# Two products of 256 columns become one of 512 in the cross attentions' key and query projections

## What is computed

```python
def memory_cross_attention(xn, mem, mem_gain, wq, wkv, wo):
    mn = rms_norm(mem, mem_gain)
    q = jnp.einsum('bsd,de->bse', xn, wq)            # 1024 -> 512, 4 heads of 128
    k, v = jnp.split(jnp.einsum('bmd,de->bme', mn, wkv), 2, axis=-1)
    s = jnp.einsum('bqhd,bkhd->bhqk', q, k) * (XA_HEAD_DIM ** -0.5)
    p = jax.nn.softmax(s, axis=-1)
    o = jnp.einsum('bhqk,bkhd->bqhd', p, v)
    return jnp.einsum('bse,ed->bsd', o, wo)

# reference(): for each of the 2 layers, behind the even or the odd mixer
x = x + memory_cross_attention(rms_norm(x, xa_norm[layer]), mem, xa_mem_norm[layer],
                               xa_wq[layer], xa_wkv[layer], xa_wo[layer])
```

## Time and profile before

| | us |
|---|---|
| median of 3 runs | 592.36 (592.31 to 592.51) |
| the profiled execution | 592.32 |
| its span in the trace | 590.5 |
| outside the span | 1.8 |
| PE busy | 578.7 (98%) |
| PE weight loads busy | 533.7 (90%) |
| DVE busy | 415.5 (70%) |
| ACT busy | 390.6 (66%) |

### The profile page before, as it was taken

The page is one execution under the profiler, slowest core; times in us unless marked ns, Lnnn a source line. Parts: engine busy times, 40 slices in busy tenths (PEclk is TensorE's granted clock), DMA queues, the critical chain, the costliest instruction groups (busy, mean ns, idle before and its releaser), DMA issues.

```text
span 590.5 us, 9701 instructions
## 1 busy us (share of the span) xinstructions
PE 578.7 (98%) x3879; PEld 533.7 (90%) x3879; DVE 415.5 (70%) x639; ACT 390.6 (66%) x587; POOL 62.2 (11%) x55
## 2 busy tenths in 40 slices
PE   7999999999999999999999999999999999999995
PEld 6999989999999898889988999999899998788984
DVE  6779589447855784567557874788998973776664
ACT  7763685278367875657666847769849828566754
POOL 7230005001001000100000001104120200100002
PEclk9999999999999999999999999999999999999999
DMA  9756354445715563464335555236544563256201
GB/s 286 251 182 224 102 184 143 143 143 214 229 58 172 165 235 142 159 231 181 143 144 170 186 172 187 85 137 224 189 150 144 181 239 132 93 213 231 89 1 71
DMA packets 51980, 97.83 MB, mean 166 GB/s; under 512 B 1372, under 2 KB 7776, under 8 KB 51936
## 3 DMA queue, kind: packets, MB, share of 16 engines
q1 hardware_dynamic: 51392, 96.87, 48.2%
q10 hardware_dynamic: 160, 0.27, 0.1%
q0 software_dynamic: 384, 0.08, 0.1%
HBM read 96.16 MB, written 1.05 MB: 165 GB/s over the span
## 4 chain that ended last, share of the span: by engine, by line
PE 80%; ACT 7%; DVE 6%; DVEq 2%; ACTq 2%; issue 1%; DMA 1%
PE proj L1705 13%; PE proj L1707 13%; PE proj L1706 13%; PE proj L1724 9%; PE proj L1726 9%; PE proj L1725 9%; PE head L1874 3%; DVE w_lo L1040 3%; ACT w_hi L476 2%; PE head L1952 1%; PE head L1762 1%; DVEq L1552 1%; ACT z_silu L514 1%; ACTq L516 1%; DVE v_rows L1501 1%
## 5 line engine op out<-in xcount | busy, mean ns | idle before, releaser
L1040 DVE TENSOR_TENSOR w_lo<-raw_weights,w_hi 128x1024 fp32r<-128x1024 f32 x174 | 227.5, 1321 | 108.1 <-ACT w_hi L476 105.7
L476 ACT ACTIVATE w_hi<-raw_weights 128x1024 fp32r<-128x1024 f32 x176 | 184.5, 1057 | 113.5 <-PE proj L1707 59.9
L1705 PE MATMUL proj<-xT_hi,w_hi 128*128 128x256 f32 x760 | 218.2, 287 | 0.2 <-DVE w_lo L1111 0.2
L1707 PE MATMUL proj<-xT_hi,w_lo 128*128 128x256 f32 x760 | 215.0, 283 | 0.0
L1706 PE MATMUL proj<-xT_lo,w_hi 128*128 128x256 f32 x760 | 215.0, 283 | 0.0
L1705 PEld LDWEIGHTS proj<-xT_hi,w_hi 128*128 128x128 f32 x760 | 145.7, 192 | 1.0 <-issue 0.3
L1706 PEld LDWEIGHTS proj<-xT_lo,w_hi 128*128 128x128 f32 x760 | 145.8, 192 | 0.6
L1707 PEld LDWEIGHTS proj<-xT_hi,w_lo 128*128 128x128 f32 x760 | 145.7, 192 | 0.0
L1724 PE MATMUL proj<-w_hi,y_hi 128*128 128x512 f32 x176 | 69.6, 396 | 0.5 <-DVE w_lo L1040 0.5
L1726 PE MATMUL proj<-w_lo,y_hi 128*128 128x512 f32 x176 | 68.6, 390 | 0.0
L1725 PE MATMUL proj<-w_hi,y_lo 128*128 128x512 f32 x176 | 68.5, 389 | 0.0
(11 more groups left out here) (277 smaller groups left out, 750.7 us busy)
## 6 DMA issues: line engine op xcount, KB each, us to landing
raw_weights<-in_ev_w_in_dram SPq DMA_DIRECT2D x15, 2048.0 KB, 8.8
raw_weights<-in_od_w_in_dram SPq DMA_DIRECT2D x12, 2048.0 KB, 8.0
raw_weights<-in_ev_w_out_dram SPq DMA_DIRECT2D x4, 2048.0 KB, 7.7
raw_weights<-in_xa_wkv_dram SPq DMA_DIRECT2D x4, 2048.0 KB, 7.8
raw_weights<-in_od_w_out_dram SPq DMA_DIRECT2D x4, 2048.0 KB, 7.7
raw_weights<-in_xa_wq_dram SPq DMA_DIRECT2D x2, 2048.0 KB, 9.0
raw_weights<-in_xa_wo_dram SPq DMA_DIRECT2D x2, 2048.0 KB, 7.8
raw_weights<-in_ev_w_in_dram SPq DMA_DIRECT2D x4, 512.0 KB, 7.9
```

The costliest lines, as they stand in the source:

```text
L476: act.activation(ring_quarter(w_hi, n, q), raw_quarter(n, q), ACT.Copy).then_inc(hi_ready, 1)
L1040: dve.tensor_tensor(ring_quarter(w_lo, n, q), raw_quarter(n, q), ring_quarter(w_hi, n, q).bitcast(F32), ALU.subtract).then_inc(lo_ready, 1)
L1705: pe.matmul(dst, wh[:, k, :], x_hi[:, k, :], start=(k == 0), stop=False)
L1707: last = pe.matmul(dst, wl[:, k, :], x_hi[:, k, :], start=False, stop=(k == KC - 1))
```

## The change

The key and query slabs of both cross attentions (four slabs) become "paired". The two parts of x lie side by side in one tensor, and for each block PE does one product of 512 columns, w_hi with x_hi and x_lo, into the two halves of a bank, and one of 256 columns, w_lo with x_hi, into the first half. So a quarter fills a whole bank, and a key slab takes four banks instead of two. The sum of the two halves is made by DVE (`tensor_reduce` over an innermost axis of 2) when the bank is read; ACT's copies of keys and queries are gone. The sums stand in DVE's order behind the `ahead` step of the same place.

```diff
+PAIRED = {("XA0", "k"), ("XA0", "q"), ("XA1", "k"), ("XA1", "q")}
...
-        _t += 2 if _kind == "W" or (_stage[:2] == "XA" and _part == "q") else 1
+        _t += 2 if _kind == "W" or is_paired(_n) else 1
...
+        xT = sb("xT", [P, 2, KC, S], F32R)
+        xT_hi, xT_lo = xT[:, 0], xT[:, 1]
...
-                copy_bank(nk, 0, kx[:, 0:2, :].rearrange("p h t -> p (h t)"), k_rows)
...
-                copy_bank(nk, 1, kx[:, 2:4, :].rearrange("p h t -> p (h t)"), k_rows)
...
-                    query(nq, h)
...
+            def pair_sum(n, half, dst, s):
+
+                filled(dve, n, 0, half)
+                dve.tensor_reduce(dst, two_banks(n, half).rearrange("p u (l t) -> p u t l", l=2), AX_X, ALU.add
+                                  ).then_inc(s, 1)
+                dve.drain().then_inc(free_of(n, 0, half), 1)
+                dve.nop().then_inc(free_of(n, 1, half), 1)
+
+            def keys_sum(n, half):
+                pair_sum(n, half, kx[:, 2 * half:2 * half + 2, :], k_rows)
+
+            def query_sum(n, h):
+
+                dve.wait_ge(quarter_used, 4 * n + h + 1)
+                dve.tensor_reduce(blocks(0)[:, h, :], bank(n, h % 2, h // 2).rearrange("p (l t) -> p t l", l=2), AX_X,
+                                  ALU.add).then_inc(q_rows, 1)
+                dve.drain().then_inc(free_of(n, h % 2, h // 2), 1)
...
-                for q in range(1, 4):
-                    ahead(nk, q)
+                ahead(nk, 1)
+                ahead(nk, 2)
+                keys_sum(nk, 0)
+                ahead(nk, 3)
                 xT_low(1, "xa_norm", 0)
                 ahead(nq, 0)
+                keys_sum(nk, 1)
                 ahead(nq, 1)
+                query_sum(nq, 0)
                 ahead(nq, 2)
+                query_sum(nq, 1)
                 softmax_max(8 + 1, 0, False)
                 ahead(nq, 3)
+                query_sum(nq, 2)
                 softmax_max(8 + 2, 1, False)
                 softmax_norm(16 + 2, 0, False)
                 ahead(nv, 0)
+                query_sum(nq, 3)
                 softmax_max(8 + 3, 2, False)
...
                 ahead(nq, 0)
+                query_sum(nq, 0)
+                ahead(nq, 1)
+                query_sum(nq, 1)
                 softmax_max(12 + 1, 0, False)
-                ahead(nq, 1)
                 softmax_norm(24 + 2, 0, False)
                 softmax_max(12 + 2, 1, False)
                 ahead(nq, 2)
+                query_sum(nq, 2)
                 softmax_max(12 + 3, 2, False)
                 softmax_norm(24 + 4, 1, False)
                 softmax_norm(24 + 6, 2, False)
+                query_sum(nq, 3)
                 cross_low(11, 0)
...
+                    if paired and k < KC - 1:
+                        pe.matmul(both, wh[:, k, :], x_pair[:, :, k, :], start=(k == 0), stop=False)
+                        pe.matmul(dst, wl[:, k, :], x_hi[:, k, :], start=False, stop=False)
```

More of the change, by code:

```diff
@@ L66, in slab, with is_paired @@
     return [n for n, s in enumerate(SLABS) if s[0] == stage and s[1] == part and s[3] == g][0]
+PAIRED = {("XA0", "k"), ("XA0", "q"), ("XA1", "k"), ("XA1", "q")}
+def is_paired(n):
+    return SLABS[n][:2] in PAIRED
 TURN = {}
@@ L96, in hybrid_trunk @@
         w_lo = sb("w_lo", [P, 4, 1024], F32R)
[L97 to L100, removed]
+        xT = sb("xT", [P, 2, KC, S], F32R)
+        xT_hi, xT_lo = xT[:, 0], xT[:, 1]
+        y = sb("y", [P, 2, 2 * KC, S], F32R)
+        y_hi, y_lo = y[:, 0], y[:, 1]
         x_sb = sb("x_residual", [P, T, D])
@@ L141, in hybrid_trunk @@
         kx = scan_mask[:, :].rearrange("p (h t) -> p h t", h=4)
-        proj = [ctx.enter_context(nc.psum_tensor(f"proj{i}", [P, 512], F32)) for i in range(4)]
+        proj_banks = ctx.enter_context(nc.psum_tensor("proj", [P, 4, 512], F32))
+        proj = [proj_banks[:, i, :] for i in range(4)]
         head = [ctx.enter_context(nc.psum_tensor(f"head{i}", [P, 512], F32)) for i in range(4)]
@@ L300, in filled, with two_banks @@
                 return
-            eng.wait_ge(quarter_used, 4 * n + (2 * u + 2 if kind == "F" else 2 * half + 2 if kind == "W" else 4))
+            eng.wait_ge(quarter_used, 4 * n + (2 * half + 2 if kind == "W" or is_paired(n) else
+                                               2 * u + 2 if kind == "F" else 4))
+        def two_banks(n, half):
+            b = 2 * ((TURN[n] + half) % 2)
+            return proj_banks[:, b:b + 2, :]
         def y_src(i):
@@ L708, in cross_high @@
                                ACT.Copy).then_inc(y_hi_ready, 1)
[L710 to L713, removed]
             def first_cross():
@@ L769, in last_cross @@
                 cross_high(1, 0)
-                query(nq, 3)
                 turned_probs(12 + 3, 2, 512)
@@ L840, in _ @@
             ahead(n, 2)
-            copy_bank(n, 0, kx[:, 0:2, :].rearrange("p h t -> p (h t)"), k_rows)
             ahead(n, 3)
@@ L894, in stage_c @@
                     silu_of_c(0)
-                else:
-                    n = slab("XA1", "k")
-                    copy_bank(n, 1, kx[:, 2:4, :].rearrange("p h t -> p (h t)"), k_rows)
                 ahead(cx, 1)
@@ L1484, in _ @@
             norm_rows(3, x_sb, W[:, 0:2, :])
-            for q in range(1, 4):
-                ahead(n, q)
+            ahead(n, 1)
+            ahead(n, 2)
+            keys_sum(n, 0)
+            ahead(n, 3)
             xT_low(2, "od_norm", 0)
@@ L1529, in stage_c @@
                 ahead(cx, 0)
+                if g == 0:
+                    keys_sum(slab("XA1", "k"), 1)
                 ahead(cx, 1)
@@ L1687, in take_bank, with quarter_f @@
                     pe.wait_ge(free_of(n, u, half), before)
-            def quarter_f(n, q, x_hi=xT_hi, x_lo=xT_lo, norm=None, four_banks=False, ks=range(KC)):
-                if four_banks:
+            def quarter_f(n, q, x_pair=xT, norm=None, ks=range(KC)):
+                x_hi, x_lo = x_pair[:, 0], x_pair[:, 1]
+                paired = is_paired(n)
+                if paired:
                     u, half, col = q % 2, q // 2, 0
@@ L1700, in quarter_f @@
                 dst = bank(n, u, half)[:, col:col + S]
+                both = bank(n, u, half).rearrange("p (a t) -> p a t", a=2)
                 wh, wl = ring_quarter(w_hi, n, q), ring_quarter(w_lo, n, q)
@@ L1704, in quarter_f @@
                         pe.wait_ge(xT_lo_ready, KC * norm + k + 1)
-                    pe.matmul(dst, wh[:, k, :], x_hi[:, k, :], start=(k == 0), stop=False)
-                    pe.matmul(dst, wh[:, k, :], x_lo[:, k, :], start=False, stop=False)
-                    last = pe.matmul(dst, wl[:, k, :], x_hi[:, k, :], start=False, stop=(k == KC - 1))
+                    if paired and k < KC - 1:
+                        pe.matmul(both, wh[:, k, :], x_pair[:, :, k, :], start=(k == 0), stop=False)
+                        pe.matmul(dst, wl[:, k, :], x_hi[:, k, :], start=False, stop=False)
+                    elif paired:
+                        pe.matmul(dst, wl[:, k, :], x_hi[:, k, :], start=False, stop=False)
+                        last = pe.matmul(both, wh[:, k, :], x_pair[:, :, k, :], start=False, stop=True)
+                    else:
+                        pe.matmul(dst, wh[:, k, :], x_hi[:, k, :], start=(k == 0), stop=False)
+                        pe.matmul(dst, wh[:, k, :], x_lo[:, k, :], start=False, stop=False)
+                        last = pe.matmul(dst, wl[:, k, :], x_hi[:, k, :], start=False, stop=(k == KC - 1))
                 if ks[-1] == KC - 1:
@@ L1746, in last_products, with slab_f @@
                     last.then_inc(last_filled, 1)
-            def slab_f(n, qs=range(4), x=(xT_hi, xT_lo), norm=None):
+            def slab_f(n, qs=range(4), x_pair=xT, norm=None):
                 for q in qs:
-                    quarter_f(n, q, x[0], x[1], norm=norm if q == 0 else None)
+                    quarter_f(n, q, x_pair, norm=norm if q == 0 else None)
             def slab_t(n, qs=range(4), x=(xT_hi, xT_lo), k0=0, start=True, stop=True):
@@ L1975, in first_cross @@
                 pe.wait_ge(mn_lo_ready, KC)
-                slab_f(nk, [0, 1, 2], x=(y_hi, y_lo))
+                slab_f(nk, [0, 1, 2], y)
                 turn_rows(W[:, 0:2, :], 2)
-                slab_f(nk, [3], x=(y_hi, y_lo))
+                slab_f(nk, [3], y)
                 for q in range(4):
-                    quarter_f(nq, q, norm=1 if q == 0 else None, four_banks=True)
+                    quarter_f(nq, q, norm=1 if q == 0 else None)
                     if q >= 1:
@@ L2006, in query @@
                 def query(q, ks=range(KC)):
-                    quarter_f(nq, q, norm=3 if q == 0 else None, four_banks=True, ks=ks)
+                    quarter_f(nq, q, norm=3 if q == 0 else None, ks=ks)
                 query(0)
@@ L2047, in _ @@
             pe.wait_ge(mn_lo_ready, 2 * KC)
-            slab_f(slab("XA1", "k"), [0, 1, 2], x=(y_hi, y_lo))
+            slab_f(slab("XA1", "k"), [0, 1, 2], y)
             turn_rows(W[:, 0:2, :], 3)
```

(2 more changed lines are left out.)

3 lines of the change are left out of this document (removed).

## The result

The changed kernel takes 594.96 us (median of 6 runs, 594.77 to 595.22), the kernel before 592.39 us beside it (592.31 to 592.71). The ratio is 1.0041 with a 95% interval of 1.0031 to 1.0052: slower by 2.6 us. The forecast was 594.8 us.

A forecast was written before the change was run, and what follows sets the result against it. PE, busy for 98% of the span, was taken to bound the kernel. First cross attention +1.0, second layer's keys +0.25 and last cross attention +1.15 gave +2.4 us on 592.32: 594.7, forecast 594.8, range 592.4 to 598.0.

The forecast's parts named there:

- a query sum, a key sum: DVE's new reductions: 0.68 us per query quarter, 1.22 us per pair of key banks, taken from the lower bound.
- score 0, first layer: First cross attention: the query sum queues behind DVE work, so PE stalls 0.8 us and starts this score at 287.11.
- score 3, first layer: First cross attention's second stall: sum queued behind softmax and `w_lo`; start 298.93 instead of 298.02, PE at +1.0 us with restart.
- PE at score 2, last layer: Last cross attention: query sum behind a `w_lo` ends at 563.64; score starts 0.84 us later, +0.94 with restart.
- and at score 3: Last cross attention: DVE's sum takes 0.68 us instead of ACT's 0.38, 0.2 us later; +1.15 us for this layer.
- The slow reduction: Rival: one more cycle per output, sums of 0.95 and 1.75 us; some +3.2 us more, 598 us; 17%.
- The restart: At scores that waited, restarting costs PE another 0.1 us: 1.13 us against 1.03.
- PE's gain: Key and query slabs: one 512-column product replaces two of 256, saving 13.3 ns per block, 1.7 us in all.
- Second layer's keys: First key sum delays `xT_low`, so PE waits at C x: the slab's 0.43 us gain lost and 0.25 more.
- PE's waits would name `xT_low` here: Sign: PE's waits name `xT_low` before C x in the second layer; the prediction is wrong if missing.
- Stages C and D: Their chain through ACT and DVE, some 50 us, starts from PE's end of C z and only moves along.

The follow-up runs named there:

- the kernel that sums nothing: Changed kernel with all four slabs paired, but DVE sums nothing and ACT copies only the first half of each bank: 591.47 us, ratio 0.9987.
- the quarters sorted by width: Reordered kernel with the last query quarter as before the change, plus whole quarters' products ordered by width instead of alternating: 591.74 us.
- XA1 k: Only the second layer's key slab is paired, the other three slabs as in the kernel before: ratio 1.0026 against that kernel.
- The reordered kernel: Changed kernel with DVE's query sums moved ahead of `w_lo` steps of the same place, and second-layer `xT_low` ahead of the third `w_lo`: 591.75 us, ratio 0.9987.
- another kernel with the same beginning: Changed kernel with each of the eight query sums done twice, one behind the other: 601.01 us.
- three kernels: Kernel before with one slab paired: first layer's keys, first layer's queries, or second layer's keys; ratios 1.0014, 1.0064 and 1.0026.
- a fourth: Kernel before with only the second layer's query slab paired: ratio 1.0026.

## Why the prediction was right

The chain of the argument held, from place to place. As it was put, and as measured:

| step of the prediction | forecast, us | measured, us |
|---|---|---|
| a query sum, a key sum | 0.68, 1.22 | 0.685, 1.218 |
| score 0, first layer, starts at | 287.11 | 287.14 |
| PE's start-to-start delay at score 0, first layer | 0.83 | 0.56 |
| score 3, first layer, starts at | 298.93 | 298.99 |
| PE at score 2, last layer, from the start of that slab | +0.94 | +0.92 |
| and at score 3 | +1.15 | +1.18 |
| in all | +2.4 | +2.5 |

**The price of a sum.** The bound from the reductions to 2 and 4 outputs was the value itself: the number of outputs (2, 4, 256) does not show in the duration of a reduction of 512 elements. The slow reduction is out.

**The restart.** Counting 0.1 us for each score that waited was right: the next product starts 0.78 us behind such a score (287.92) and 0.68 behind one that didn't wait (286.92 to 287.60 in the kernel before). At score 3 it turns the +0.92 of the table into +1.03, for 1.0 in the forecast.

**PE's gain was mis-sized.** The step was "13.3 ns gained for each block of inputs", 1.7 us in all. It is 1.0 us in the kernel that sums nothing, 8 ns for each of the 128 blocks. The fixed part of a product is nearly right, as the quarters sorted by width show (2.77 and 2.80 us); in turns of 512 and 256 columns a pair takes 351 and not 347 ns in most quarters. The error hardly reached the sum: at four scores and at C x the time was set by DVE, and there PE's gain is only the length of its wait. PE came to score 0 at 286.58 (its last product started at 286.35) and not at 286.28, and so waited less; the score started when it was said to. The rule of the Trainium skill ("TensorE: Matmul & The Clock Gate", section "Back-to-back issue gap"), which is given there for a single product by itself and by which a block would gain 2.5 ns and all of them an estimated 0.3 us, leaves too little here: 8 ns was measured.

**Second layer's keys.** I had 0.25 us for the slab and its wait at C x together; alone it is +0.31 (XA1 k in the table), in the changed kernel +0.21 from the keys to the last query slab. PE loses it in two parts:

```profile
337.27 0.40 PE L1744 MATMUL proj<-y,w_hi 128*128 128x512 f32 x1
337.77 0.36 PE L1746 MATMUL proj<-xT,w_hi 128*128 128x256 f32 x1
...
338.93 0.32 PE L1746 MATMUL proj<-xT,w_hi 128*128 128x256 f32 x1
...
339.32 0.32 PE L1746 MATMUL proj<-xT,w_hi 128*128 128x256 f32 x1
```

C x starts 0.50 us behind the last key product, where 0.23 is the distance behind a product of 512, since `xT_low` begins only at 337.15 and takes 0.4 us for its first block; and it reads blocks at the pace of `xT_low`, 0.39 us apart instead of 0.36. The prediction said that PE's waits would name `xT_low` here, and that it would be wrong if they did not. The list does not name it: the delays are small beside the overlapping durations of the products. The mechanism is shown by these distances and by the next kernel, not by that sign. The reordered kernel, which has `xT_low` ahead of a `w_lo`, is free of it (-0.53 to -0.77 over that slab).

**Score 3 of the first layer.** That ACT without its copy would come to the same place, since the maximum in front of its exponential is later, was right: `w_lo` started at 297.11, 297.0 in the forecast.

**Stages C and D** move along as said: no row of the tables changes by more than 0.27 us between C x and the last query slab, and that is the wait inside C x.

## What to carry to other kernels

Before moving work from one engine to another that has idle time, look at what stands in front of it in the new queue and how soon the reader comes; here the same instructions made the kernel 2.5 us slower or 0.6 us faster than before, by whether weight splits that nobody needed yet stood in front of the sums and of `xT_low` or behind them. Count a saving on the bounding engine only up to its next wait for another engine: in the changed kernel nothing was left of PE's 1.0 us, in the reordered one 0.6. And compare two kernels by the starts of the same instructions along the span, not by the totals: that showed four steps of known size where the total would once have spoken for the wrong theory. It also shows what a list of waits leaves out: a result that comes just as its reader arrives still cost 0.1 us.

## What the runs showed of the hardware

- Between fp32r products of one width, the distance is 120.0 ns at 256 columns and 226.7 ns at 512 in the long stretches read for the prediction. It is not so everywhere: in the changed kernel eleven products of 512 columns from 295.67 to 297.98 us are 231 ns apart. In turns a pair takes 351 ns in most quarters, 4 to 5 more than the sum; the quarter behind the transposes took 348 (six pairs from 278.51 to 280.60). Why one and not the other is open. Since products of 512 columns alone also differ by 4 ns from place to place, the change of width is not shown to be the whole cause; the sorted first key slab shows it for 0.1 us.
- A reduction over pairs of columns 256 apart, from PSUM, takes 0.685 us for 512 elements and 1.218 us for 1024. Reductions of 512 elements to 2 and to 4 outputs take 0.686 to 0.689 us.
- A score of four products takes 1.12 to 1.13 us instead of 1.02 to 1.03 when it had to wait, and the next product starts 0.1 us later behind it.
- At the start of the kernel ACT began its first `w_hi` at 7.64 us in one traced execution and, held up by the transfer of the weights, at 9.83 us in another kernel with the same beginning; the anchor of the table moved by the same 2.2 us. The time outside the span was 1.7 to 1.9 us in most runs and 2.4 to 2.9 us in nearly all of three kernels and three runs of a fourth. Both are as large as the effects studied here, and no run ties either to the edits.
